# A hybrid encoder layer: projections begun with two token tiles, norm rows spread by TensorE, and loads and zero fills put elsewhere

## The reference

```python
z = layer_norm(x, ln_in_g, ln_in_b)
q, k, v, xr, gr, gl = split(z @ w_in)        # 512, 128, 128, 1024, 1024, 2048 columns
q, k = partial_rope(q), partial_rope(k)
attn = sink_attention(q, k, v)               # chunked, 64 queries at a time
xc = causal_conv(xr)                         # width 4
r, i = sigmoid(blocks(xc) @ w_rg_a + b_a), sigmoid(blocks(xc) @ w_rg_x + b_x)   # 8 blocks of 128
h = scan(a(r), u(i, xc)); rnn = h * gelu(gr)
mix = (sigmoid(gl_a) * (attn @ w_pa) + sigmoid(gl_r) * (rnn @ w_pr)) @ w_o
z1 = layer_norm(ALPHA * z + mix)
y = layer_norm(ALPHA * z1 + hier_moe(z1))    # 16 experts, 2 per token
```

## Time and profile before

| | us |
|---|---|
| runs | 635.85, 643.37, 639.69; median 639.69 |
| the profiled execution's own time | 645.62 |
| its span, first to last instruction | 643.8 |
| mean granted TensorE clock | 0.919 |
| busy: PE, DVE, ACT, POOL | 531.8, 229.8, 130.2, 71.1 |

### The profile page before, as it was taken

The page is one execution under the profiler, slowest core; times in us unless marked ns, Lnnn a source line. Parts: engine busy times, 40 slices in busy tenths (PEclk is TensorE's granted clock), DMA queues, the critical chain, the costliest instruction groups (busy, mean ns, idle before and its releaser), DMA issues.

```text
span 643.8 us, 9041 instructions
## 1 busy us (share of the span) xinstructions
PE 531.8 (83%) x3544; PEld 393.8 (61%) x3545; DVE 229.8 (36%) x487; ACT 130.2 (20%) x240; POOL 71.1 (11%) x88
## 2 busy tenths in 40 slices
PE   1299979999999999999992699978987789787740
PEld 1299965987888897968772456544554455444310
DVE  5623985685344222213336111121111111111177
ACT  1424359654423122100020000000000000000010
POOL 4590400000000000010000700010000000000210
PEclk9999998977999999999975599998988999989795
DMA  7696541212135887891066269999999999999632
GB/s 216 193 235 224 150 131 54 84 61 65 34 131 186 312 281 273 285 329 69 33 254 252 80 255 374 389 398 393 390 386 412 409 408 406 409 424 424 236 122 82
DMA packets 55353, 158.53 MB, mean 246 GB/s; under 512 B 3572, under 2 KB 35792, under 8 KB 51216
## 3 DMA queue, kind: packets, MB, share of 16 engines
q1 hardware_dynamic: 46320, 135.11, 55.9%
q0 software_dynamic: 4896, 13.92, 8.0%
q10 hardware_dynamic: 4096, 8.92, 3.8%
HBM read 146.14 MB, written 11.78 MB: 245 GB/s over the span
## 4 chain that ended last, share of the span: by engine, by line
PE 61%; DMA 20%; DVE 7%; issue 4%; ACT 3%; SPq 3%; DVEq 0%; POOL 0%; POOLq 0%; ACTq 0%
PE bank L1015 19%; DMA expert_slots<-in_w_up 10%; PE bank L825 8%; PE bank L976 7%; PE bank L812 6%; PE bank L814 6%; PE bank L813 6%; DMA expert_slots<-in_w_in 5%; PE bank L901 3%; SPq L591 2%; PE bank L1008 2%; DMA z_rows<-work 2%; PE bank L881 1%; DVE work L1384 1%; DMA expert_slots<-expert_rows,slot_i 1%
## 5 line engine op out<-in xcount | busy, mean ns | idle before, releaser
L1015 PE MATMUL bank<-expert_slots,work 128*64 128x256 f32 (+3 forms) x1584 | 191.7, 416 | 26.1 <-DMA expert_slots<-in_w_gate 11.1
L1015 PEld LDWEIGHTS bank<-expert_slots,work 128*64 128x64 f32 (+1 forms) x1584 | 106.7, 139 | 100.0 <-issue 45.8
L812 PE MATMUL bank<-z_high,weights_high 128*128 128x320 f32 (+1 forms) x256 | 81.5, 318 | 0.6 <-DVE weights_low L532 0.6
L813 PE MATMUL bank<-z_low,weights_high 128*128 128x320 f32 (+1 forms) x256 | 79.9, 312 | 0.0
L814 PE MATMUL bank<-z_high,weights_low 128*128 128x320 f32 (+1 forms) x256 | 79.8, 312 | 0.0
L1720 DVE SCALAR_TENSOR_TENSOR work<-work,bank 128x256 f32<-128x256 f32 (+1 forms) x18 | 7.3, 406 | 144.0 <-ACT work L1296 138.1
L532 DVE TENSOR_TENSOR weights_low<-expert_slots,weights_high 128x2048 fp32r<-128x2048 f32 x18 | 41.2, 2287 | 34.0 <-ACT weights_high L527 34.0
L825 PE MATMUL bank<-work,expert_slots 128*128 128x320 f32 x192 | 52.3, 432 | 0.0
L812 PEld LDWEIGHTS bank<-z_high,weights_high 128*128 128x128 f32 x256 | 48.9, 191 | 1.9 <-DVE weights_low L532 1.1
L813 PEld LDWEIGHTS bank<-z_low,weights_high 128*128 128x128 f32 x256 | 48.6, 190 | 0.2
L814 PEld LDWEIGHTS bank<-z_high,weights_low 128*128 128x128 f32 x256 | 48.5, 189 | 0.0
(11 more groups left out here) (249 smaller groups left out, 590.8 us busy)
## 6 DMA issues: line engine op xcount, KB each, us to landing
expert_slots<-in_w_gate SPq DMA_DIRECT2D x16, 2048.0 KB, 25.0
expert_slots<-in_w_up SPq DMA_DIRECT2D x16, 2048.0 KB, 29.6
expert_slots<-in_w_down SPq DMA_DIRECT2D x15, 2048.0 KB, 23.5
expert_slots<-in_w_in SPq DMA_DIRECT2D x19, 1024.0 KB, 5.6
expert_slots<-in_w_branch_rnn SPq DMA_DIRECT2D x4, 1024.0 KB, 7.3
expert_slots<-in_w_out SPq DMA_DIRECT2D x4, 1024.0 KB, 5.7
expert_rows<-work ACTq DMA_DIRECT2D x30, 128.0 KB, 8.2
expert_rows<-work POOLq DMA_DIRECT2D x6, 384.0 KB, 9.3
```

Source lines behind the costliest of these rows:

```text
L812: nc.tensor.matmul(b[:, 0:NALL - lo], wh[:, k, o], zh[:, k, lo:NALL], start=(k == 0), stop=False)
L813: nc.tensor.matmul(b[:, 0:NALL - lo], wh[:, k, o], zl[k // 4][:, k % 4, lo:NALL], start=False, stop=False)
L1015: mm = nc.tensor.matmul(bank[m * j:m * j + m, cols], lhsT(k), rhs(k, j), start=(k == 0), stop=(k == kk - 1))
```

## The change

- SP loads tile 0, then only the first 257 columns of the constants (identity, ones, epsilon, which the table now puts first), tile 1, unit 0, the two parts of tile 2, units 1 and 2, and then the other constants.
- The norm rows come as two DMAs to one partition; PE spreads them with four matmuls of a row of ones (one row of contraction, 128 by 512 each), ACT copies them out.
- The block weights have a place of their own in `work` (`w_rg`, which `rnnT` takes over later) and are issued behind unit 5; there is no unit 7 for them, so all later units have numbers one lower, and each of the `gr` units 1 and 2 waits for an earlier one than before.
- PE turns tiles 0 and 1, and the nine groups run in the order of `QKV_ORDER`; tile 2 is normed by DVE after the first two units are split, and turned just ahead of its own first group. DVE splits unit 0.
- POOL zeroes first, waits for the second split before it loads the caches, and issues the 22 fills last of its early work, behind a wait for `conv_made` of 2.

```diff
-U_QKV, U_XR, U_RG, U_GR, U_MERGE, U_OUT = 0, 3, 7, 8, 12, 28
+U_QKV, U_XR, U_GR, U_MERGE, U_OUT = 0, 3, 7, 11, 27
...
+QKV_ORDER = ((0, 0), (1, 0), (0, 1), (2, 0), (1, 1), (2, 1), (0, 2), (1, 2), (2, 2))
...
+        w_rg = work[:, area.at:area.at + UNIT].rearrange("p (w n e) -> p w n e", w=2, e=P)
         rnnT = area.take(KD, NTOK)
...
             sp.dma_start(rows[:, 0, :], xp[0:P, :]).then_inc(x_in[0], 16)
-            sp.dma_start(const[:], t["const"]).then_inc(const_in, 16)
+            first = CC["eps"][1]
+            sp.dma_start(const[:, 0:first], t["const"][:, 0:first]).then_inc(const_in, 16)
             sp.dma_start(rows[:, 1, :], xp[P:2 * P, :]).then_inc(x_in[1], 16)
...
-            for u in range(EARLY):
+            unit(0)
+            sp.dma_start(rows[0:DEC, 2, :], xs).then_inc(x_in[2], 16)
+            sp.dma_start(rows[DEC:DEC + META, 2, :], t["meta_tokens"]).then_inc(x_in[2], 16)
+            unit(1)
+            unit(2)
+            sp.dma_start(const[:, first:NCONST], t["const"][:, first:NCONST]).then_inc(tables_in, 16)
+            for u in range(3, EARLY):
                 unit(u)
+                if u == U_XR + 2:
+                    for w, name in enumerate(("w_rg_a", "w_rg_x")):
+                        sp.dma_start(w_rg[:, w], t[name][0].rearrange("n c e -> c n e")).then_inc(rg_in, 16)
...
+            nc.gpsimd.memset(merged[:, 0:4, :].rearrange("p k n -> p (k n)")[:, 0:D], 0.0).then_inc(zeroed, 1)
...
+            pool.wait_ge(low_made, 2)
             pool.dma_start(kW, t["cache_win_k"][0, 0].rearrange(flat)).then_inc(cache_in, 16)
...
-            low_of(pool, SPLIT[0], nc.gpsimd)
-
-            nc.gpsimd.memset(merged[:, 0:4, :].rearrange("p k n -> p (k n)")[:, 0:D], 0.0).then_inc(zeroed, 1)
-            pool.wait_ge(zeroed, 1)
-            zeros = merged[0:REST, 0:4, :].rearrange("p k n -> p (k n)")[:, 0:D]
-            for i in range(NE):
...
             pool.dma_start(br[:, NG:20], t["b_router"].rearrange("a g e -> a (g e)")).then_inc(router_in, 16)
+            pool.wait_ge(zeroed, 1)
+            pool.wait_ge(conv_made, 2)
+            zeros = merged[0:REST, 0:4, :].rearrange("p k n -> p (k n)")[:, 0:D]
+            for i in range(NE):
+                pool.dma_start(y_dram[CAP * i + FIRST:CAP * (i + 1), :], zeros).then_inc(zero_out, 16)
...
+            pe.wait_ge(scale_in, 32)
+            for i in range(2):
+                for h in range(2):
+                    b = S.claim(pe, ("scale", i, h))
+                    nc.tensor.matmul(b[:, :], ones[0:1, :], gb[0:1, i, 512 * h:512 * h + 512], start=True, stop=True)\
+                        .then_inc(S.f_full(("scale", i, h)), 1)
+            turn_tokens(0)
+            turn_tokens(1)
+            for j, u in QKV_ORDER:
...
+                if (j, u) == (2, 0):
+                    turn_tokens(2)
...
-            norm_rows_load("ln_in_g", "ln_in_b")
+            for i, name in enumerate(("ln_in_g", "ln_in_b")):
+                act.dma_start(gb[0:1, i, :], t[name].rearrange("(o d) -> o d", o=1)).then_inc(scale_in, 16)
             act.wait_ge(const_in, 16)
+            for i in range(2):
+                for h in range(2):
+                    b = S.arrived(act, ("scale", i, h))
+                    nc.scalar.copy(gb[:, i, 512 * h:512 * h + 512], b[:, :]).then_inc(S.f_free(("scale", i, h)), 1)
...
+            token_norm(0)
+            token_norm(1)
+            token_low(0)
+            low_of(dve, SPLIT[0])
             token_low(1)
+            low_of(dve, SPLIT[1])
+            token_norm(2)
             token_low(2)
-            dve.wait_ge(low_made, 1)
-            low_of(dve, SPLIT[1])
             low_of(dve, SPLIT[2])
             low_of(dve, SPLIT[3])
```

More of the change, by code:

```diff
@@ L72, in const_layout @@
     cols, at = {}, 0
-    for name, n in (("ident", P), ("before", P), ("ones", P), ("cos", 3 * HALF), ("sin", 3 * HALF),
+    for name, n in (("ident", P), ("ones", P), ("eps", 1), ("before", P), ("cos", 3 * HALF), ("sin", 3 * HALF),
                     ("iota_cap", CAP), ("iota_item", NITEM), ("iota_ov", NOV), ("expert", NE),
-                    ("tie", 4), ("token", 3), ("valid", 3), ("eps", 1)):
+                    ("tie", 4), ("token", 3), ("valid", 3)):
         cols[name] = (at, at + n)
@@ L209, in pe_fills @@
     m, s = [], []
+    s += [("scale", i, h) for i in range(2) for h in range(2)]
     for j in range(3):
         s += [("zT", j, h) for h in range(2)]
-    m += [("qkv", j, u) for u in range(3) for j in range(3)]
+    m += [("qkv", j, u) for j, u in QKV_ORDER]
     s.append("vec")
@@ L563, in unit @@
                 wide = dst.rearrange("p (k n) -> p k n", n=256)
[L564 to L568, removed]
-                    col = 256 * u if u < U_RG else C_GR + 256 * (u - U_GR)
+                if u < U_MERGE:
+                    col = 256 * u if u < U_GR else C_GR + 256 * (u - U_GR)
                     sp.dma_start(wide, w_in[:, :, col:col + 256]).then_inc(done, 16)
@@ new lines, in _ @@
+                if u == 0:
+                    for h in range(2):
+                        S.emptied(pe, ("zT", j, h))
+                b = M.claim(pe, ("qkv", j, u))
+                wh, wl = parts(u)
+                for k in range(KD):
+                    z = slice(at, at + n)
+                    nc.tensor.matmul(b[0:n, 0:256], zh[:, k, z], wh[:, k, :], start=(k == 0), stop=False)
+                    nc.tensor.matmul(b[0:n, 0:256], zh[:, k, z], wl[:, k, :], start=False, stop=False)
+                    mm = nc.tensor.matmul(b[0:n, 0:256], zl[k // 4][:, k % 4, z], wh[:, k, :], start=False, stop=(k == KD - 1))
@@ L800, in _ @@
+                mm.then_inc(M.f_full(("qkv", j, u)), 1)
             pe.wait_ge(vec_in, 128)
@@ L1380, in normed @@
             def normed(i, j, n):
-                if j == 0:
-                    dve.wait_ge(norm_in, 32 * (i + 1))
+                if j == 0 and i == 0:
+                    for w in range(2):
+                        for h in range(2):
+                            S.emptied(dve, ("scale", w, h))
+                elif j == 0:
+                    dve.wait_ge(norm_in, 32 * i)
                 dve.wait_ge(var_ready, 3 * i + j + 1)
```

87 lines of the change are left out of this document (34 added, 53 removed).

## The result

| | before | after |
|---|---|---|
| median of 13 runs each (lowest to highest), us | 643.28 (635.85 to 644.68) | 637.86 (636.53 to 640.64) |
| the profiled execution's own time, its span, us | 645.62, 643.8 | 637.03, 635.2 |

The ratio of the runs is 0.9945 (0.9920 to 0.9971): the change makes the kernel faster by 0.3 to 0.8%, 3.5 us with an interval of 1.9 to 5.1, where I forecast 0.9 us more. The medians alone differ by 5.4 us (0.9916). Ratios and their intervals leave out runs over 1.5% above the fastest of their kernel; medians keep them. The profiled pair differs by 8.6 us, because the profiled execution of before was slower than all of its 13 runs.

What follows compares the result with a forecast made beforehand. Bounds: the start, and ACT's r and i stage behind the second gr unit. Gains of 5.7 and 1.38 us, eaten by 8.0, left 0.9 us more: 639.7 + 0.9 = 640.6 us, range 631.5 to 645.5.

Steps and rivals of the forecast that it cites:

- The start: From the first loads to the first xr matmul: that matmul at 52.1 us, 5.7 us earlier, bounds 10 and 1.
- the spread: Four PE matmuls spreading the norm rows before tile 0's norm: 1.75 us each, 7.0 us in all.
- the break for tile 2: PE waits ahead of tile 2's first group while it is turned and taken apart: 2.0 us, from 0.8 to 2.5.
- Doubling a late matmul's time: Spread matmuls at the start: 0.88 us late in the kernel, doubled to 1.75 for the clock's lower level.
- caches, late constants or block weights: Loads costed at nothing, as wanted long after issue; were one cover gone, its price would be 5 to 12 us.
- The demand: ACT ready for the second gr unit 34.0 us after the first xr matmul; unit issued 22.4 us after it.
- POOL's queue is full all that time: Fills keep POOL's queue full from 20.4 to 39.2 us after the first xr matmul.
- one for one, the unit's 1,024 packets outlast them: Second gr unit shares packets equally with some 880 of the fills, landing 42.0 us after the first xr matmul.
- ACT's forecast wait of 8.0 us: Before the r and i stage: second gr unit comes 8.0 us later than wanted, stage begins at 94.1 us.
- the first rival: Second gr unit gets through beside the fills before ACT wants it: 7.1 us earlier, 632.6 us; chance 0.20.
- The rival that held: Fills leave SP's queue its share, so the second gr unit causes no wait: 7.1 us earlier, 632.6; chance 0.20.
- both tiles' norm behind the last spread row: DVE norms tiles 0 and 1 after the last copy at 12.5 us: 6.8 plus 0.3 us, done at 19.6.

Runs made afterwards that it cites:

- old_start: Kernel before with only the block weights outside the ring and the 22 fills behind the second convolved block: median 640.32 us, ratio to before 0.9954.
- big_fills_first: Changed kernel with the six fills of 96 rows issued ahead of the sixteen of 32 rows: median 644.63 us, ratio to before 1.0017.
- rg_in_ring: Changed kernel with the block weights back in the ring as unit 7, so later units have their old numbers: 650.36 us, ratio to before 1.0106.
- issued_before: Changed kernel with all 22 fills issued ahead of the key and value outputs, large ones first: 644.25 us, ratio to before 0.9996.
- issue_slowly: big_fills_first with six small waited-for POOL writes behind each 32-row fill, slowing the issue: 641.20 us, ratio to before 0.9956.
- fills_earlier: Changed kernel without POOL's wait for the second convolved block, same fills issued 3.7 us earlier: 637.89 us, ratio to before 0.9930.
- split_norm: Changed kernel with tiles 0 and 1's statistics and roots ahead of the copies, products per spread row, unit 0 split before the turned tiles: 633.12 us, ratio to before 0.9832.
- fills_old_place: Changed kernel with the 22 fills back beside the q, k, v groups, behind the cache loads: 643.98 us, ratio to before 1.0035.
- roots_apart: split_turn with tile 1's root behind the copies of the scale row instead of ahead of them: 632.62 us, ratio to before 0.9848.
- split_turn: split_norm with tile 2 turned one group earlier, ahead of the third group: 632.48 us, ratio to before 0.9809.
- vectors_later: roots_apart with POOL's ten small loads behind unit 0's split instead of at the start: 630.74 us, ratio to before 0.9824.

## Why the prediction was wrong

**The start was right.** Constants at 4.67 us (5 taken, of which no row gave the 3 us until bytes flow), the spread 7.19 (7.0), tile 0's norm at 12.73 (12.5), first projection at 23.21 (23.2), the break for tile 2 2.4 (2.0), first xr matmul at 52.66 (52.1). Doubling a late matmul's time for a PE that had stood idle was right to 0.2 us. The cause I gave, the lower of the clock's two levels, fits the pace of the projections that follow (start, length):

```profile
27.22 0.41 PE L811 MATMUL bank<-weights_high,z_high 128*128 128x256 f32 x1
27.43 0.41 PE L812 MATMUL bank<-weights_low,z_high 128*128 128x256 f32 x1
...
27.83 0.28 PE L811 MATMUL bank<-weights_high,z_high 128*128 128x256 f32 x1
27.94 0.28 PE L812 MATMUL bank<-weights_low,z_high 128*128 128x256 f32 x1
```

Matmuls of one shape start 0.21 us apart until 27.7 us and 0.11 apart from then on. The trace's first record of the clock begins there, at the upper level; for the time before it there is none, and the 1.00 that the profile gives for 0 to 26 us is no measurement. POOL's split had indeed held DVE up: DVE's first step on tile 2 took 3.77 us beside it before, in `old_start` too, and 1.28 in the changed kernel. No wait of an engine in the first 120 us is for caches, late constants or block weights.

**The demand was right.** ACT was ready for the second gr unit at 86.48, 33.8 us after the first xr matmul (34.0), and the unit was issued 22.4 us after it, as taken.

**The step that failed** is "POOL's queue is full all that time", and with it "one for one, the unit's 1,024 packets outlast them". From 74 to 77 us POOL's queue moved 0.50 MB, about the four fills issued before the unit; then the unit went ahead with 950 packets against 173, and the later fills had to wait. It landed at 84.4, 31.7 us after the first xr matmul and not 42.0, and ACT's forecast wait of 8.0 us was none. An exchange of one packet for one was measured where all fills stood issued: 493 against 495 behind it in the same trace, 530 against 501, 612 against 520 and 550 against 620 in three runs. I had read it from queues among the experts (18 and 16 packets) and from unit 3 (27 against 72), which met a full queue, and carried it to a unit that arrives among the first fills. I even wrote the difference down, as what speaks for the first rival, and gave it 0.20.

With the large fills first the forecast's time comes out: 42.0 us after a first xr matmul at 52.5 is 94.5, and ACT got the unit at 94.79. That shows a hold-up of that size, brought back by the order of the fills alone. That the number agrees so well is partly luck, since the parts differ: the unit stood behind the large fills until 80 us, had more than two packets to one until 85 and one for one only then, and fills were still moving when it landed.

**The rival that held** gave 7.1 us at the stage; it was 6.7. It gave 632.6 for a median of 639.7 that later runs put at 643.3; of its 7.1 us the medians show 5.4 and the ratio 3.5, where by the table's slope 6.0 were to come. That 637.9 lies near my 640.6 is luck: on the median of 643.3 the forecast would have read 644.2. The gather before the experts still stood 7.1 us earlier in the profiled pair (its first matmul at 353.35 against 360.44), so nothing is lost up to there; behind it the two profiled executions differ by 1.5 us more (8.6 in the span), which is within what one kernel's runs differ.

The Trainium skill (DMA: Bandwidth & Descriptors, section Queues, rings and completion order) has an engine go round its queues by packets, each of which holds several descriptors. I had taken each of the profile's packets for one such turn, and no run here shows how much a turn holds: both 950 against 173 and 493 against 495 are compatible with the rule.

Why the share changes stays open. That fills give way while POOL issues them fits the changed kernel, `big_fills_first`, `rg_in_ring` and `issued_before`. It does not fit `issue_slowly` from 84 to 85 us (76 against 78 with POOL still issuing) or `fills_earlier` from 82 to 84 (352 against 130 behind the last issue), and the one run meant to change the issue alone changed the queue's length too.

**What bounds the changed kernel's start** are terms that the forecast had at their size, both tiles' norm behind the last spread row. Taking them apart (`split_norm`) was worth another 4.7 us by medians and 5.5 by the stage, of which 3.4 are the norm's order and 2.1 PE's pace in that execution.

## What to carry to other kernels

A rate at which two queues share holds for the state in which it was read: note how much stood issued in each when the second one came, and price a load first by what is ahead of it then. Whether it also has to share with what is issued while it moves depends on more than these runs explain: 32-row fills gave way in one order (950 to 173) and not in the other (520 to 612), so try it. Bulk writes with a late deadline belong behind the last load that somebody waits for (not tried here), or in small pieces issued while that load moves; moving a start forward and leaving them in its way can lose all of the gain at the next load (`fills_old_place`). When an idle engine takes over a spread, let each consumer wait for its own row of it, not for all.

## What the runs showed of the hardware

- The packets of a load (rows of 1 KB) and of DRAM writes (rows of 4 KB and short records) went 5.5 to 1 while POOL was still issuing the writes (950 to 173), 2.4 to 1 with large writes ahead (475 to 194), and near 1 to 1 in five stretches behind the last issue (495 to 493, 501 to 530, 520 to 612, 620 to 550, and 445 to 496 in fills_old_place from 43 to 50 us). There are exceptions both ways: 76 to 78 with issues still to come, 352 to 130 behind the last one.
- In two runs a unit moved in bulk once the fills issued ahead of it had moved: 0.50 MB moved for 0.52 issued in the changed kernel, 1.61 for 1.57 in fills_earlier.
- PE's projections of one shape followed by 0.21 us until 27.7 us and by 0.11 after in the changed kernel. In split_norm and roots_apart they followed by 0.12 almost from the first, in split_turn and vectors_later by 0.21 for some 4 us. One execution each: what decides it was not tried.
- With ACT's square root ahead of the copies, one table load of 1.28 us stood in ACT's start instead of two: the copies needed none of their own.
- PE's granted clock from 150 to 180 us was 1.00, the upper of its two levels throughout, in fills_old_place, where PE had stood for 6.4 us ahead of the xr groups, and 0.89 before; its gather came 259.2 us after the stage against 265.5. One execution each: that the pause gave it was not tried.
